# Four k-tile steps for the first projection block, with input quarters and weight halves loaded in turn

## The chip, the cores and the metric

The kernel runs on one core of one Trainium2 chip. The metric is the device time of one execution in microseconds (us). TensorE (PE) does the products and the transposes, with its weight loads shown apart (PEld); VectorE (DVE), ScalarE (ACT) and GpSimd (POOL) do the rest, and SyncE (SP) issues most of the DMAs.

## What is computed

Four layers over a sequence of 256 tokens with 2048 features, all in float32: a mixer of dilated window attention, latent attention (both with a layer norm behind them), and two layers of a second block. Only the very start of the first layer is touched:

```python
cos_a, sin_a = rope_tables(positions, DSA_HEAD_DIM)
h = x @ w_in                                   # (256, 2048) @ (2048, 20480)
qkv = h[..., :3 * DSA_GROUPS * DSA_WIDTH].reshape(B, S, DSA_GROUPS, 3, DSA_HEADS, DSA_HEAD_DIM)
q = apply_rope(qkv[:, :, g, 0], cos, sin)
k = apply_rope(qkv[:, :, g, 1], cos, sin)
o, l = dilated_window_attention(q, k, qkv[:, :, g, 2], window, dilation)
```

## The kernel before

Every product is made of float32 numbers split into a high and a low part: for input and weights alike, `hi` is the rounded copy and `lo` is what is left of the original. The input `x` (tokens on the partitions) is transposed on TensorE into 16 k-tiles of 128 features by 256 tokens. This is `turn_x`: a group g is two k-tiles, so four 128x128 transposes into one bank of the accumulator memory (L660). ACT copies the group to `xh` (L1230) and raises a count, and DVE then makes `xl` (L1810) and raises the count `xt_d`. There are eight groups; two of them come from one quarter of `x`.

Weights come in units of 1 MB, each loaded by two DMAs of 512 KB, its halves, into one of four places of `raw`. A half h goes through `split(h)`: ACT copies it to `whi` (L1200) as soon as the unit is there and place h mod 4 is free (`half_done`), and DVE subtracts to get `wlo` (L1779) and raises `lo_done`. ACT and DVE are three halves ahead of TensorE (`AHEAD`). In the first product of layer 0, `block_by_rows`, a half holds 4 k-tiles of 256 columns: 4 x 2 products with `whi` (L621, 512 wide, against `xh` and `xl` together) and as many with `wlo` (L620, and L623 for the first k-tile). Four halves (0 to 3) make the first block of 16 k-tiles; halves 4 to 7 make the second, and so on. Half h is waited for by `lo_done`, and the first block also waits for `xl` of groups 0 to 3 before half 0 and of groups 4 to 7 before half 2 (L609, L610).

Each engine runs its own program in order; side work is interleaved by hand. A generator (`tables` in the first pair) stands beside the products, and each half lets it take two steps: on TensorE one after two of the four k-tiles and one at the end, on ACT and DVE right behind `split(h + 3)`. The seventh step holds on TensorE the transposes of the vectors (L759, L760), on DVE their copy to `vec` (L1960) and then the whole chain of angles for the rope tables (L1962 to L1990), and on ACT the wait for that chain and the sines (L1348 to L1352). For DVE and ACT the seventh step stands behind `split(6)`. After the sines ACT copies the first block out (L1396), and only then comes `split(7)`. On POOL the seven mask operations (L2536, L2558) wait for the last of DVE's six small mask operations (L2041 to L2044).

At the start SP issues the four quarters of `x` (L562), then eleven small DMAs of rows of vectors (L567), then the weights (L572). TensorE, ACT and DVE do all eight groups of `turn_x`, DVE then the six mask operations, and ACT and DVE then `split(0)` to `split(2)`. The wait of `split(0)` is for both halves of unit 0, since `loaded` counts them together.

Of the kernel before, what the change touches and what calls it, by code (L numbers as in the profile page):

```python
# [10 lines left out]
ALU = mybir.AluOpType  # L11
# [3 lines left out]
P = 128  # L15
# [6 lines left out]
NEG = -1e30  # L22
# [46 lines left out]
def turns(n):  # L69
    for _ in range(n):  # L70
        yield
# [87 lines left out]
def build_program(nc, a, out, layers=(0, 1, 2, 3)):  # L159
    assert tuple(layers) == (0, 1, 2, 3)  # L160
    ctx = ExitStack()
    with ctx:
# [7 lines left out]
        def sem(name):  # L170
            return ctx.enter_context(nc.semaphore(name))

        raw = sb("raw", [P, 4, 4, N])
# [36 lines left out]
        raw_in = [sem(f"raw_in{j}") for j in range(4)]  # L210
        hi_done, lo_done, half_done = sem("hi_done"), sem("lo_done"), sem("half_done")
        x_in = [sem(f"x_in{q}") for q in range(4)]
        x_out = [sem(f"x_out{q}") for q in range(4)]
        vec_in, tab_in = sem("vec_in"), [sem("pos_in"), sem("inv_in")]
        ln_in, l2_in, l3_in = [sem("lng_in"), sem("lnb_in")], [sem("relb_in"), sem("ifb_in")], \
# [6 lines left out]
        m0_g = marks("m0_g", "iota zero band*7")  # L222
        m0_d = marks("m0_d", "bits0 low0 high0 bits1 low1 high1")
        xt_p, xt_a, xt_d = marks("xt_p", "t"), marks("xt_a", "hi"), marks("xt_d", "lo")
# [59 lines left out]
        class L0:  # L284
            c = Carve()
            h = c(10, TB, HALF)
# [13 lines left out]
            bits = flat(t2)[:, 0:S].bitcast(I32)  # L300
# [253 lines left out]

        loaded = [0] * 4
        for n_, (_, parts_) in enumerate(weights()):
            loaded.append(loaded[n_] + 16 * len(parts_))


        def sync(sp):  # L560
            for q in range(4):
                sp.dma_start(x[:, :, q * N:(q + 1) * N],  # L562
                             a["x"][0].rearrange("(t p) d -> p t d", p=P)[:, :, q * N:(q + 1) * N]).then_inc(x_in[q], 16)
            sp.wait_ge(*setup_d.at(0, "zero"))
            for name, src, n in rows:
                g, o = places[name] // P, places[name] % P
                sp.dma_start(vrows[o:o + n, g, :], src).then_inc(vec_in, 16)  # L567
            for u, (_, halves) in enumerate(weights()):
                if u >= 4:
                    sp.wait_ge(lo_done, 2 * (u - 4) + 2)  # L570
                for dst, src in halves:
                    sp.dma_start(dst(raw[:, u % 4]), src).then_inc(raw_in[u % 4], 16)  # L572
            for q in range(4):
                sp.wait_ge(*add_d.at(3, f"add{q}"))
                sp.dma_start(out[0].rearrange("(t p) d -> p t d", p=P)[:, :, q * N:(q + 1) * N],
                             x[:, :, q * N:(q + 1) * N]).then_inc(x_out[q], 16)
            for q in range(4):
                sp.wait_ge(x_out[q], 16)


        def tensor(pe):
# [23 lines left out]
            def block_by_rows(side, bank, wait_x):  # L605


                for u in range(2):
                    if wait_x:  # L609
                        pe.wait_ge(*xt_d.at(4 * u + 3, "lo"))  # L610
                    for s in range(2):
                        h = half[0]
                        pe.wait_ge(lo_done, h + 1)
                        hi, lo = block_half(whi[:, h % 4]), block_half(wlo[:, h % 4])
                        for t in range(4):
                            k = 8 * u + 4 * s + t
                            for c in range(2):
                                cols = slice(c * P, (c + 1) * P)
                                if k:
                                    pe.matmul(ps[:, bank + c, 0:S], lo[:, t, cols], xh[:, k, :], start=False, stop=False)  # L620
                                m = pe.matmul(ps[:, bank + c, :], hi[:, t, cols], xx[:, :, k, :], start=k == 0, stop=k == KT - 1)  # L621
                                if k == 0:
                                    m = pe.matmul(ps[:, bank + c, 0:S], lo[:, t, cols], xh[:, k, :], start=False, stop=False)  # L623
                            if t == 1:
                                next(side, None)
                        m.then_inc(half_done, 1)
                        half[0] += 1
                        next(side, None)
# [34 lines left out]
            def turn_x(layer, groups=range(8)):  # L663
                for g in groups:
                    if layer in (1, 2) or g % 2 == 0:
                        pe.wait_ge(*x_there(layer, g))
                    if g >= 4:
                        pe.wait_ge(*xt_d.at(8 * layer + g - 4, "lo"))
                    four(4 + g % 4, lambda l, tb: x[:, tb, (2 * g + l) * P:(2 * g + l + 1) * P]).then_inc(*xt_p.up("t"))
# [134 lines left out]
                return beside(paced(heads0(pair - 1), 3) if pair else tables_, 54, paced(rope0(pair), 3))  # L804

            pe.wait_ge(*const.at(0, "ident"))
            turn_x(0)
            for pair in range(8):
                side = beside0(pair, tables())
                for s in range(8):  # L810
# [378 lines left out]
        def scalar(act):  # L1189
            half = [0]  # L1190

            def split(h):
                if h >= 2 * len(widths):
                    return
                u = h // 2
                act.wait_ge(raw_in[u % 4], loaded[u + 4])
                if h >= 4:
                    act.wait_ge(half_done, h - 3)
                n = widths[u]
                act.copy(whi[:, h % 4, :, 0:n] if n > FEW else few_high(h, n),  # L1200
                         whole_half(raw[:, u % 4, 2 * (h % 2):2 * (h % 2) + 2], n)).then_inc(hi_done, 1)
# [178 lines left out]
            def beside0(pair, tables_):  # L1380
                return beside(paced(heads0(pair - 1), 3) if pair else tables_, 54, paced(rope0(pair), 3))

            turn_x(0)
            for h in range(AHEAD):
                split(h)
            for pair in range(8):
                side = beside0(pair, tables())
                for s in range(8):
                    b = bank0(s)
                    if s < 6:  # L1390
                        unit(side)
                        unit(side)
                        act.wait_ge(half_done, half[0])
                        if pair:
                            act.wait_ge(*p0_d.at(pair - 1, f"r{s}"))
                        act.copy(L0.h[:, s], ps[:, b:b + 2, 0:S]).then_inc(*e0_a.up(f"out{s}"))  # L1396
                        continue
                    project(side, then=turning_y(0) if pair + s == 14 else None)
                    act.wait_ge(half_done, half[0])
                    if s == 6:  # L1400
                        act.copy(L0.h[:, 6:8].rearrange("p b t c -> p t b c"),
                                 ps[:, b:b + 2, :].rearrange("p t (b c) -> p t b c", b=2)).then_inc(*e0_a.up("out6"))
                    else:
                        if pair:
                            act.wait_ge(*p0_d.at(pair - 1, "z"))
                        act.copy(L0.h[:, 8], ps[:, b:b + 2, 0:HALF])
                        act.activation(L0.h[:, 9], ps[:, b:b + 2, HALF:N], ACT.Copy, scale=0.5).then_inc(*e0_a.up("out7"))
                run(side)
# [361 lines left out]
        def vector(dve):  # L1770
# [184 lines left out]


            def tables():
                yield from turns(6)
                dve.wait_ge(*setup_p.at(0, "vec"))
                dve.tensor_copy(vec[:, :], ps[:, 7, 0:2 * P]).then_inc(*setup_d.up("vec"))  # L1960
                dve.wait_ge(tab_in[0], 16)
# [71 lines left out]
                return beside(paced(heads0(pair - 1), 3) if pair else tables_, 54, paced(rope0(pair), 3))  # L2033

            dve.memset(vrows, 0.0).then_inc(*setup_d.up("zero"))
            turn_x(0)
            dve.wait_ge(*m0_g.at(0, "zero"))
            for i, dil in enumerate((4, 16)):
                if i:
                    dve.wait_ge(*m0_d.at(0, "high0"))  # L2040
                dve.tensor_scalar(L0.bits, L0.iota, dil - 1, None, ALU.bitwise_and).then_inc(*m0_d.up(f"bits{i}"))  # L2041
                dve.wait_ge(*m0_d.at(0, f"bits{i}"))
                dve.tensor_scalar(L0.m0[:, i + 1], L0.bits[:, 0:P], 1.0, NEG, ALU.min, ALU.mult).then_inc(*m0_d.up(f"low{i}"))
                dve.tensor_scalar(L0.m1[:, i + 1], L0.bits, 1.0, NEG, ALU.min, ALU.mult).then_inc(*m0_d.up(f"high{i}"))  # L2044
            for h in range(AHEAD):
                split(h)
            for pair in range(8):
                side = beside0(pair, tables())
                for s in range(8):
                    if s < 6:  # L2050
                        unit(side)
                        unit(side)
                        dve.wait_ge(*e0_a.at(pair, f"out{s}"))
                        dve.tensor_tensor(L0.h[:, s], L0.h[:, s], ps[:, bank0(s):bank0(s) + 2, S:N], ALU.add) \  # L2054
                            .then_inc(*s0_d.up(f"sum{s}"))
                    else:
                        project(side, then=turning_y(0) if pair + s == 14 else None)
                run(side)
# [656 lines left out]
```

## Time and profile before

| what | value |
|---|---|
| median of 3 runs | 2478.17 us (2474.19 to 2478.46) |
| the profiled execution | 2472.55 us |
| its span | 2470.8 us |
| mean granted TensorE clock | 0.995 |
| PE busy | 98% of the span |
| DVE, ACT, POOL busy | 59%, 48%, 6% |

The span runs from the first instruction to the last; 1.75 us of the execution lie around it. Times in the rows are microseconds from the start of the span, durations in a group are means, and what stands in brackets is the idle time of the engine before the row and what ended it. A granted clock of 1.00 is 2.4 GHz and 0.50 is 1.2 GHz.

### The profile page before, as it was taken

The numbers are of one execution on the slowest core, as the hardware profiler recorded it, in microseconds if no ns is written. First come the engines' busy times: TensorE is split into PE (matmuls) and PEld (weight loads), VectorE is DVE, ScalarE is ACT, GpSimd is POOL, SyncE is SP. The second block draws the span as 40 slices with busy tenths as digits, with TensorE's granted clock in tenths as the row PEclk, the third lists the DMA queues.
The fourth block names the chain that finished last, engine by engine and source line by source line (L and its number), as shares of the span: only waits on it lengthen the run. The fifth ranks groups of instructions, "written<-read, shape, count | busy, mean of one in ns | idle before, by whom it ended". The sixth has DMA issues, their size and how long they took to land.

```text
span 2470.8 us, 31396 instructions
## 1 busy us (share of the span) xinstructions
PE 2426.0 (98%) x12674; PEld 2063.6 (84%) x12674; DVE 1469.1 (59%) x1932; ACT 1190.8 (48%) x1620; POOL 152.2 (6%) x127
## 2 busy tenths in 40 slices
PE   8999999999999999989999989999999999999999
PEld 7888888888888888878899878888888887888887
DVE  5757574757475747565556566554455566757654
ACT  4444444444444444445555445555444468655443
POOL 1101010101010101000000000000000010000000
PEclk9999999999999999999999999999999999999999
DMA  7555555545554555546554545555555564433344
GB/s 241 180 174 174 171 183 166 191 160 188 164 191 156 187 163 178 201 142 194 170 137 137 204 147 187 171 187 173 185 169 161 167 205 156 138 116 120 103 137 136
DMA packets 367141, 414.58 MB, mean 168 GB/s; under 512 B 27722, under 2 KB 298276, under 8 KB 366484
## 3 DMA queue, kind: packets, MB, share of 16 engines
q1 hardware_dynamic: 365588, 405.63, 51.5%
q0 software_dynamic: 1408, 6.94, 0.8%
q8 instruction: 100, 1.64, 0.3%
q14 instruction: 45, 0.37, 0.0%
HBM read 410.42 MB, written 2.10 MB: 167 GB/s over the span
## 4 chain that ended last, share of the span: by engine, by line
PE 90%; DVE 4%; ACT 3%; issue 1%; DMA 1%; SPq 0%; POOL 0%; ACTq 0%; DVEq 0%
PE ps L593 18%; PE ps L595 18%; PE ps L594 18%; PE ps L621 14%; PE ps L620 7%; PE ps L1071 2%; DVE wlo L1779 1%; PE ps L660 1%; PE ps L795 1%; ACT whi L1200 1%; PE ps L782 1%; PE ps L787 1%; PE ps L844 1%; PE ps L845 1%; PE ps L846 1%
## 5 line engine op out<-in xcount | busy, mean ns | idle before, releaser
L1779 DVE TENSOR_TENSOR wlo<-raw,whi 128x1024 fp32r<-128x1024 f32 (+1 forms) x768 | 946.7, 1242 | 679.6 <-ACT whi L1200 677.5
L1200 ACT CAST whi<-raw 128x1024 fp32r<-128x1024 f32 (+1 forms) x774 | 801.9, 1041 | 746.9 <-PE ps L595 566.4
L593 PE MATMUL ps<-whi,xx 128*128 128x512 f32 x2112 | 842.1, 399 | 0.7 <-DVE wlo L1779 0.7
L595 PE MATMUL ps<-whi,xx 128*128 128x512 f32 x2112 | 824.0, 390 | 0.0
L594 PE MATMUL ps<-wlo,xx 128*128 128x512 f32 x2112 | 822.6, 389 | 0.0
L621 PE MATMUL ps<-xx,whi 128*128 128x512 f32 x1536 | 540.9, 397 | 5.4 <-DVE wlo L1779 5.4
L595 PEld LDWEIGHTS ps<-whi,xx 128*128 128x128 f32 x2112 | 396.4, 188 | 84.6
L593 PEld LDWEIGHTS ps<-whi,xx 128*128 128x128 f32 x2112 | 396.9, 188 | 79.3 <-DVE wlo L1779 1.4
L594 PEld LDWEIGHTS ps<-wlo,xx 128*128 128x128 f32 x2112 | 397.2, 188 | 77.5
L620 PE MATMUL ps<-xx,wlo 128*128 128x256 f32 x1440 | 406.7, 282 | 0.4 <-DVE wlo L1779 0.4
L621 PEld LDWEIGHTS ps<-xx,whi 128*128 128x128 f32 x1536 | 286.9, 188 | 69.5 <-issue 5.6
L620 PEld LDWEIGHTS ps<-xx,wlo 128*128 128x128 f32 x1440 | 272.2, 189 | 2.9 <-DVE wlo L1779 0.7
L2568 POOL TENSOR_TENSOR work<-work 128x512 f32<-128x512 f32 x48 | 101.7, 2118 | 844.3 <-DVE work L2011 654.8
L1299 ACT ACTIVATE work<-work,small 128x128 f32<-128x128 f32 (+1 forms) x80 | 46.1, 577 | 154.9 <-DVE small L1933 154.9
L2007 DVE TENSOR_TENSOR work<-work 64x512 f32<-64x512 f32 x96 | 88.5, 921 | 2.2
L2054 DVE TENSOR_TENSOR work<-work,ps 128x512 f32<-128x512 f32 x48 | 32.9, 686 | 39.6 <-ACT work L1396 39.6
L1396 ACT COPY work<-ps 128x512 f32<-128x512 f32 x48 | 28.0, 583 | 57.5 <-PE ps L621 57.5
L1071 PEld LDWEIGHTS ps<-work 128*128 128x128 f32 x384 | 49.6, 191 | 7.0 <-DVE work L2414 3.5
L1930 DVE CUSTOM_DVE_ANT_0 work<-ps,work 128x128 f32<-128x128 f32 (+1 forms) x80 | 38.2, 515 | 24.3 <-PE ps L782 18.5
L1071 PE MATMUL ps<-work 128*128 128x128 f32 x384 | 51.1, 276 | 1.4 <-DVE work L2414 1.3
L844 PE MATMUL ps<-xx,whi 128*128 128x256 f32 x160 | 49.0, 306 | 0.0
L846 PE MATMUL ps<-xx,whi 128*128 128x256 f32 x160 | 45.2, 282 | 0.0
(401 smaller groups left out, 1830.5 us busy)
## 6 DMA issues: line engine op xcount, KB each, us to landing
raw<-in_dsa_w_in SPq DMA_DIRECT2D x320, 512.0 KB, 4.5
raw<-in_ev_w_in SPq DMA_DIRECT2D x144, 512.0 KB, 4.6
raw<-in_od_w_in SPq DMA_DIRECT2D x96, 512.0 KB, 4.5
raw<-in_mla_w_in SPq DMA_DIRECT2D x48, 512.0 KB, 4.5
raw<-in_dsa_w_out SPq DMA_DIRECT2D x32, 512.0 KB, 4.6
raw<-in_mla_w_out SPq DMA_DIRECT2D x32, 512.0 KB, 4.8
raw<-in_ev_w_out SPq DMA_DIRECT2D x32, 512.0 KB, 4.5
raw<-in_od_w_out SPq DMA_DIRECT2D x32, 512.0 KB, 4.9
```

The lines of the kernel that those rows point to most:

```text
L593: pe.matmul(o, xh[:, k, tokens[tb]], hi, start=start and s + l == 0, stop=False)
L594: pe.matmul(o, xh[:, k, tokens[tb]], lo, start=False, stop=False)
L595: m = pe.matmul(o, xl[:, k, tokens[tb]], hi, start=False, stop=stop and s + l == 2)
L620: pe.matmul(ps[:, bank + c, 0:S], lo[:, t, cols], xh[:, k, :], start=False, stop=False)
L621: m = pe.matmul(ps[:, bank + c, :], hi[:, t, cols], xx[:, :, k, :], start=k == 0, stop=k == KT - 1)
L844: pe.matmul(o, hi, xh[:, k, :], start=first and g != 1, stop=False)
L846: m = pe.matmul(o, hi, xl[:, k, :], start=False, stop=last and g != 0)
L1071: m = pe.matmul(ps[:, bank, n * P:(n + 1) * P], left[:, n, :], right[:, n, :], start=True, stop=True)
L1200: act.copy(whi[:, h % 4, :, 0:n] if n > FEW else few_high(h, n), whole_half(raw[:, u % 4, 2 * (h % 2):2 * (h % 2) + 2], n)).then_inc(hi_do ...
L1779: dve.tensor_tensor(wlo[:, h % 4, :, 0:n] if n > FEW else few_low(h, n), whole_half(raw[:, h // 2 % 4, 2 * (h % 2):2 * (h % 2) + 2], n), h ...
L2007: m = dve.tensor_tensor(L0.t2[a_], L0.h[b_, n], bc(L0.sina[b_], 1, 2), ALU.mult)
L2568: pool.tensor_tensor(L0.t1, L0.h[:, n], bc(L0.cosa, 1, 2), ALU.mult).then_inc(*p0_g.up(f"cos{n}"))
```

## The change

SP now issues quarter 0 of `x`, half 0 of the weights, quarter 1, half 1, and so on up to half 3, each with a semaphore of its own, then the rows of vectors, then the weights from unit 2 on. `split(0)` to `split(3)` wait for their own half alone. All three engines turn only groups 0 and 1 ahead of the products. TensorE turns groups 2 and 3 after the second k-tile of half 0, groups 4 and 5 after that of half 1, and groups 6 and 7 after that of half 2. ACT and DVE do the same groups right behind `split(0)`, `split(1)` and `split(2)`. TensorE waits for `xl` group by group, before each pair of k-tiles. The six mask operations of DVE go into `tables`: three in its second step, behind `split(3)`, and three in its fourth, behind `split(4)`.

```diff
--- before.py
+++ after.py
@@ -210,6 +210,7 @@
         raw_in = [sem(f"raw_in{j}") for j in range(4)]
         hi_done, lo_done, half_done = sem("hi_done"), sem("lo_done"), sem("half_done")
         x_in = [sem(f"x_in{q}") for q in range(4)]
+        first_in = [sem(f"first_in{h}") for h in range(4)]
         x_out = [sem(f"x_out{q}") for q in range(4)]
         vec_in, tab_in = sem("vec_in"), [sem("pos_in"), sem("inv_in")]
         ln_in, l2_in, l3_in = [sem("lng_in"), sem("lnb_in")], [sem("relb_in"), sem("ifb_in")], \
@@ -554,18 +555,23 @@
 
         loaded = [0] * 4
         for n_, (_, parts_) in enumerate(weights()):
-            loaded.append(loaded[n_] + 16 * len(parts_))
+            loaded.append(loaded[n_] + (16 * len(parts_) if n_ >= 2 else 0))
 
 
         def sync(sp):
-            for q in range(4):
+
+            first = [part for _, halves in list(weights())[0:2] for part in halves]
+            for q, (dst, src) in enumerate(first):
                 sp.dma_start(x[:, :, q * N:(q + 1) * N],
                              a["x"][0].rearrange("(t p) d -> p t d", p=P)[:, :, q * N:(q + 1) * N]).then_inc(x_in[q], 16)
+                sp.dma_start(dst(raw[:, q // 2]), src).then_inc(first_in[q], 16)
             sp.wait_ge(*setup_d.at(0, "zero"))
             for name, src, n in rows:
                 g, o = places[name] // P, places[name] % P
                 sp.dma_start(vrows[o:o + n, g, :], src).then_inc(vec_in, 16)
             for u, (_, halves) in enumerate(weights()):
+                if u < 2:
+                    continue
                 if u >= 4:
                     sp.wait_ge(lo_done, 2 * (u - 4) + 2)
                 for dst, src in halves:
@@ -606,14 +612,14 @@
 
 
                 for u in range(2):
-                    if wait_x:
-                        pe.wait_ge(*xt_d.at(4 * u + 3, "lo"))
                     for s in range(2):
                         h = half[0]
                         pe.wait_ge(lo_done, h + 1)
                         hi, lo = block_half(whi[:, h % 4]), block_half(wlo[:, h % 4])
                         for t in range(4):
                             k = 8 * u + 4 * s + t
+                            if wait_x and t % 2 == 0:
+                                pe.wait_ge(*xt_d.at(k // 2, "lo"))
                             for c in range(2):
                                 cols = slice(c * P, (c + 1) * P)
                                 if k:
@@ -622,6 +628,8 @@
                                 if k == 0:
                                     m = pe.matmul(ps[:, bank + c, 0:S], lo[:, t, cols], xh[:, k, :], start=False, stop=False)
                             if t == 1:
+                                if wait_x and k < 12:
+                                    turn_x(0, (k // 2 + 2, k // 2 + 3))
                                 next(side, None)
                         m.then_inc(half_done, 1)
                         half[0] += 1
@@ -804,7 +812,7 @@
                 return beside(paced(heads0(pair - 1), 3) if pair else tables_, 54, paced(rope0(pair), 3))
 
             pe.wait_ge(*const.at(0, "ident"))
-            turn_x(0)
+            turn_x(0, (0, 1))
             for pair in range(8):
                 side = beside0(pair, tables())
                 for s in range(8):
@@ -1193,7 +1201,10 @@
                 if h >= 2 * len(widths):
                     return
                 u = h // 2
-                act.wait_ge(raw_in[u % 4], loaded[u + 4])
+                if h < 4:
+                    act.wait_ge(first_in[h], 16)
+                else:
+                    act.wait_ge(raw_in[u % 4], loaded[u + 4])
                 if h >= 4:
                     act.wait_ge(half_done, h - 3)
                 n = widths[u]
@@ -1380,9 +1391,10 @@
             def beside0(pair, tables_):
                 return beside(paced(heads0(pair - 1), 3) if pair else tables_, 54, paced(rope0(pair), 3))
 
-            turn_x(0)
+            turn_x(0, (0, 1))
             for h in range(AHEAD):
                 split(h)
+                turn_x(0, (2 * h + 2, 2 * h + 3))
             for pair in range(8):
                 side = beside0(pair, tables())
                 for s in range(8):
@@ -1955,7 +1967,17 @@
 
 
             def tables():
-                yield from turns(6)
+                yield
+                dve.wait_ge(*m0_g.at(0, "zero"))
+                for i, dil in enumerate((4, 16)):
+                    if i:
+                        dve.wait_ge(*m0_d.at(0, "high0"))
+                    dve.tensor_scalar(L0.bits, L0.iota, dil - 1, None, ALU.bitwise_and).then_inc(*m0_d.up(f"bits{i}"))
+                    dve.wait_ge(*m0_d.at(0, f"bits{i}"))
+                    dve.tensor_scalar(L0.m0[:, i + 1], L0.bits[:, 0:P], 1.0, NEG, ALU.min, ALU.mult).then_inc(*m0_d.up(f"low{i}"))
+                    dve.tensor_scalar(L0.m1[:, i + 1], L0.bits, 1.0, NEG, ALU.min, ALU.mult).then_inc(*m0_d.up(f"high{i}"))
+                    yield from turns(2)
+                yield
                 dve.wait_ge(*setup_p.at(0, "vec"))
                 dve.tensor_copy(vec[:, :], ps[:, 7, 0:2 * P]).then_inc(*setup_d.up("vec"))
                 dve.wait_ge(tab_in[0], 16)
@@ -2033,17 +2055,10 @@
                 return beside(paced(heads0(pair - 1), 3) if pair else tables_, 54, paced(rope0(pair), 3))
 
             dve.memset(vrows, 0.0).then_inc(*setup_d.up("zero"))
-            turn_x(0)
-            dve.wait_ge(*m0_g.at(0, "zero"))
-            for i, dil in enumerate((4, 16)):
-                if i:
-                    dve.wait_ge(*m0_d.at(0, "high0"))
-                dve.tensor_scalar(L0.bits, L0.iota, dil - 1, None, ALU.bitwise_and).then_inc(*m0_d.up(f"bits{i}"))
-                dve.wait_ge(*m0_d.at(0, f"bits{i}"))
-                dve.tensor_scalar(L0.m0[:, i + 1], L0.bits[:, 0:P], 1.0, NEG, ALU.min, ALU.mult).then_inc(*m0_d.up(f"low{i}"))
-                dve.tensor_scalar(L0.m1[:, i + 1], L0.bits, 1.0, NEG, ALU.min, ALU.mult).then_inc(*m0_d.up(f"high{i}"))
+            turn_x(0, (0, 1))
             for h in range(AHEAD):
                 split(h)
+                turn_x(0, (2 * h + 2, 2 * h + 3))
             for pair in range(8):
                 side = beside0(pair, tables())
                 for s in range(8):
```

## Rows read from the trace of the kernel before

**Rows 1.** The page: the span, TensorE's busy time, and the chain's shares.
```profile
span 2470.8 us, 31396 instructions
PE 2426.0 (98%) x12674; PEld 2063.6 (84%) x12674; DVE 1469.1 (59%) x1932; ACT 1190.8 (48%) x1620; POOL 152.2 (6%) x127
...
PE 90%; DVE 4%; ACT 3%; issue 1%; DMA 1%; SPq 0%; POOL 0%; ACTq 0%; DVEq 0%
```

**Rows 2.** Timeline, all engines, loads and transposes: start, length, engine, line, count, idle before.
```profile
0.81 1.97 SPq L562 DMA_DIRECT2D x<-in_x  x4
...
5.18 6.07 PE L660 MATMUL ps<-ident,x 128*128 128x128 f32 x32 [5.18 <-DMA x<-in_x]
...
6.30 0.59 ACT L1230 CAST xx<-ps 128x512 fp32r<-128x512 f32 x1 [4.22 <-PE ps L660]
...
7.16 0.59 ACT L1230 CAST xx<-ps 128x512 fp32r<-128x512 f32 x1 [0.27 <-PE ps L660]
7.44 49.48 SPq L572 DMA_DIRECT2D raw<-in_dsa_w_in  x24
...
9.72 2.20 ACT L1230 CAST xx<-ps 128x512 fp32r<-128x512 f32 x4 [0.27 <-PE ps L660]
10.16 0.86 PEld L660 LDWEIGHTS ps<-ident,x 128*128 128x128 f32 x8 [0.21 <-DMA x<-in_x]
```

**Rows 3.** The same timeline from the mask operations to the first products.
```profile
12.74 0.28 DVE L2041 TENSOR_SCALAR work<-work 128x256 int32<-128x256 int32 x1
...
13.99 0.28 DVE L2044 TENSOR_SCALAR work<-work 128x256 f32<-128x256 int32 x1
14.03 1.99 ACT L1200 CAST whi<-raw 128x1024 fp32r<-128x1024 f32 x2 [2.10 <-DMA raw<-in_dsa_w_in]
...
15.11 2.70 DVE L1779 TENSOR_TENSOR wlo<-raw,whi 128x1024 fp32r<-128x1024 f32 x2 [0.83 <-ACT whi L1200]
...
16.61 0.77 PE L621 MATMUL ps<-xx,whi 128*128 128x512 f32 x1 [5.36 <-DVE wlo L1779]
...
19.31 0.41 PE L620 MATMUL ps<-xx,wlo 128*128 128x256 f32 x1
```

**Rows 4.** The same timeline from half 2 to the rope chain's start.
```profile
24.07 1.05 ACT L1200 CAST whi<-raw 128x1024 fp32r<-128x1024 f32 x1 [1.78 <-PE ps L621]
...
26.90 1.05 ACT L1200 CAST whi<-raw 128x1024 fp32r<-128x1024 f32 x1 [1.77 <-PE ps L621]
...
27.98 1.23 DVE L1779 TENSOR_TENSOR wlo<-raw,whi 128x1024 fp32r<-128x1024 f32 x1 [1.59 <-ACT whi L1200]
...
29.12 0.42 DVE L1960 COPY vec<-ps 128x256 f32<-128x256 f32 x1
...
29.44 0.63 PE L621 MATMUL ps<-xx,whi 128*128 128x512 f32 x2
```

**Rows 5.** Timelines of single engines, 36 to 41 us: split(7), half 7, table transposes.
```profile
36.18 3.89 ACT L1200 CAST whi<-raw 128x1024 fp32r<-128x1024 f32 x4
...
37.26 4.63 DVE L1779 TENSOR_TENSOR wlo<-raw,whi 128x1024 fp32r<-128x1024 f32 x4 [0.26 <-ACT whi L1200]
...
38.54 0.38 PE L620 MATMUL ps<-xx,wlo 128*128 128x256 f32 x1 [0.38 <-DVE wlo L1779]
...
40.05 0.60 PE L765 MATMUL ps<-ident,work 128*128 128x128 f32 x4
...
40.68 0.37 ACT L1358 COPY work<-ps 128x256 f32<-128x256 f32 x1 [0.62 <-PE ps L765]
```

**Rows 6.** The POOL masks, from the timeline: start, length, count.
```profile
14.50 3.82 POOL L2536 TENSOR_SCALAR_AFFINE_SELECT work<-work 128x128 f32<-128x128 f32 x6 [10.01 <-DVE work L2044]
```

**Rows 7.** Stretches: busy time of PE, PEld, DVE, ACT, POOL; granted clock; DMA share; GB/s.
```profile
13.00:14.00 1.00, 0.00 (x0) 0.00 (x0) 0.90 (x6) 0.00 (x0) 0.00 (x0) 0.54 1.09 348
...
19.00:20.00 1.00, 1.00 (x5) 0.82 (x5) 1.00 (x2) 0.02 (x1) 0.66 (x1) 0.54 1.10 348
```

## The prediction

> **What bounds the kernel.** I read the page first: TensorE is busy 2426.0 of 2470.8 us and holds 90% of the chain that ended last [rows 1]. So only what delays TensorE counts, and almost all of the span is untouched. Next I read the timeline of the start. TensorE waits 5.18 us for the first quarter, transposes until 11.25, and then waits 5.36 us for its first product at 16.61 [rows 2, 3]. In that wait ACT idles 2.10 us for the weights, which are there at 14.03 [rows 3]. The change aims at this stretch. The reader should then look for the next place where TensorE is not fed: half 7 starts at 38.54, 0.38 us late, when `wlo` of `split(7)` is there [rows 5]. Behind that start stand, in DVE's and ACT's program order, `split(6)` at 27.98, the copy of the vectors at 29.12, the rope chain, the sines, and `split(7)` [rows 4, 5]. A time saved on TensorE before half 7 is thus worth something only if DVE also gets to the rope chain earlier; a delay of `split(6)` passes to half 7 almost in full. I count the change to that start, since from there the program and its covers are the same as before.
>
> **Loads.** Eight groups of transposes take quarters at 5.18 and, for the last, at 10.16 where TensorE waited 0.21 for it: (10.16 - 5.18) / 3 = 1.66 us for 512 KB [rows 2]. In the new order half 0 of the weights lands near 5.18 + 1.66 = 6.8, quarter 1 near 8.5, half 1 near 10.2, quarter 2 near 11.8, half 2 near 13.5, quarter 3 near 15.1 and half 3 near 16.8. SP issued a quarter each 0.5 us (four in 1.97), so the eight go out by 5 us, ahead of the engines that carry them [rows 2]. The eleven row loads go from before the weights to behind half 3; they are wanted first in half 3, about 12 us after half 3's data is there, and unit 2 is issued behind them at about the 9.5 us at which it went out before. I count the loads at nothing from here on; the cover is the slow sequence of the engines, worked out next. The four extra semaphores cost no instruction.
>
> **First product.** The casts of groups 0 and 1 stay at 6.30 and 7.16 [rows 2]. `split(0)` follows at the pitch of casts in a row, (2.20 - 0.59) / 3 = 0.54 us, at 7.70 [rows 2]. DVE starts 15.11 - 14.03 = 1.08 after it and takes 1.23 us without POOL beside it [rows 3, 4], and TensorE begins 0.1 later: 7.70 + 1.08 + 1.23 + 0.1 = 10.1 against 16.61. That is 6.5 us gained. It is almost all lost again, because in the old order half 1, 2 and 3 were ready without TensorE's help, and in the new one they are not.
>
> **Each round from half to half.** ACT's program now has groups 2 and 3 ahead of `split(1)`, and these wait for TensorE to do two k-tiles of half 0 first. So half 1 can start only after this string, of which nothing lies beside the next: two k-tiles, two groups of transposes, ACT's casts of them, ACT's `split(1)`, DVE's `split(1)`. The same holds for halves 2 and 3. At 2.4 GHz: a half takes 26.90 - 24.07 = 2.83, so two k-tiles 1.42 [rows 4]. A group's transposes take 0.86 / 2 = 0.43 [rows 2]; a cast follows the first of four transposes by 40.68 - 40.05 = 0.63 [rows 5], so the second group's cast starts at the later of 0.43 + 0.63 and 0.63 + 0.54, 1.17. `split` follows 0.54 later, DVE 1.08 after that, 1.23 long, 0.1 to TensorE: 1.17 + 0.54 + 1.08 + 1.23 + 0.1 = 4.12. One round is 1.42 + 4.12 = 5.54 us for 2.83 us of products. DVE's `xl` (0.69 each, its rows as the casts') lies beside ACT's `split`, at no cost.
>
> The first round is at 1.2 GHz, at least in its beginning: the first two k-tiles took 19.31 - 16.61 = 2.70 [rows 3], groups of transposes come 7.16 - 6.30 = 0.86 apart, the first cast 6.30 - 5.18 = 1.12 after the first transpose [rows 2]. All at that clock: 2.70 for the k-tiles and 1.12 + 0.86 + 0.54 + 1.08 + 1.23 + 0.1 = 4.93 behind them, 7.63. The clock granted at 13.0 to 14.0 fell to half, 1.8 us after the transposes ended, and rose at about 19.9, 3.3 us after the first product [rows 3, 7]. TensorE is busy without a pause from 10.1 in the new order, so a rise 3.3 us in, at 13.4, spares most of the slow transposes. 7.63 is the upper end and 7.63 - (4.93 - 4.12) = 6.82 the lower; I take 7.3. Starts: half 1 at 17.4, half 2 at 22.9, half 3 at 28.5. With half 3's products (2.83) and the two transposes of vectors (0.2), the first block ends at 31.5; before it ended at 29.44 [rows 4].
>
> **DVE on its way to the rope chain.** `split(3)` ends 0.1 before half 3, at 28.4. Before, the first six halves' splits had been done early, and `split(6)` only waited for its place. Now DVE has in a row: three mask operations, `split(4)`, three mask operations, `split(5)`, `split(6)`. Six mask operations took 13.99 + 0.28 - 12.74 = 1.53 [rows 3], which used to lie in the wait for weights and now lie on this path; a split in a row takes (4.63 - 1.23) / 3 = 1.13 [rows 5]. `split(6)` starts at 28.4 + 1.53 + 2 x 1.13 = 32.2. The end of the mask operations also starts POOL's masks, 3.82 us for six [rows 6]; beside them DVE's splits took 2.70 / 2 = 1.35 or more instead of 1.23 [rows 3], which adds 0.1 to 0.3 here. `split(6)` comes 32.4 - 27.98 = 4.4 later than before. The chain, the sines, and `split(7)` follow as before, so half 7 starts 4.4 to 4.6 later, near 43.0. TensorE is through half 6 at 31.5 + 3 x 2.83 = 40.0, so it waits 3.0 us there; the first block's own lateness (2.1) lies inside. After it ACT and DVE split four in 3.89 and 4.63 us against 11.3 us of products and are ahead again [rows 5]. I see nothing later that gives back or adds.
>
> **Sum.** +4.5 us. Bounds: 3.7 (early rise of the clock, no cost of POOL) to 5.9 (late rise, and one round with a clock that has fallen, worth 2.70 - 1.42 = 1.3 in its k-tiles and less in its transposes). On the profiled execution that is 2472.55 + 4.5 = 2477.1; on the median of the runs shown, which lies 5.6 above it, 2478.17 + 4.5 = 2482.7. Median and profiled execution differ by more than the effect, and the profile is the lowest of the four executions, so I forecast near the median's figure, 2482.
>
> **Rivals.**
> (a) The clock falls in every round. TensorE idles 4.12 - 0.86 - 1.42 = 1.8 us of each 5.54, just as long as the time from the end of the transposes to the fall seen at 13 us [rows 2, 7]; for it speaks this, against it that products of 2.8 us lie between. A slow round costs (2.70 - 1.42) + (4.93 - 4.12) = 2.1 more; rounds 2 and 3 give 4.2, so 4.5 + 4.2: 2486.9. The Trainium skill has such a rule in TensorE: Matmul & The Clock Gate, section "HAM oscillation — how this bites in real kernels": bursts too short beside their waits make every tile of a loop start throttled. No row here shows an alternation; the rule and this trace agree only in that a wait lowered the clock.
> (b) Loads don't come in turn. If the queue's transfers share the engines, so that half 0 of the weights is there only with the last quarter or later, at 14 instead of 6.8, the first product goes back to 16.6 and the rounds come on top. It decides from a landing later than 7.7. Quarters in the trace landed 1.66 apart in order of issue, which speaks against it [rows 2]. Time: + 4.5 + 6.3, 2489.
> (c) The change does what it is meant to: rounds are hidden and TensorE runs on. Then the first block is 29.44 - 16.61 = 12.83 of work, plus six groups, two at 0.86 and four at 0.43, 3.4 us: it ends at 10.1 + 12.8 + 3.4 = 26.3, 3.1 early; the rope chain starts as much earlier: 2475.1. It needs ACT to split half 1 before groups 2 and 3, and its program order says otherwise.
> (d) Only the block's lateness counts, +2.1, 2480.3, if DVE makes up its mask operations and splits before the rope chain. DVE has no idle time there in my sum, so it's unlikely.
>
> **How the numbers follow.** Forecast 0.62, (a) 0.10, (b) 0.06, (c) 0.12, (d) 0.10. A measurement of this kernel can tell about 0.2%, 5.0 us, from no change. The forecast at +3.7 to +5.9 straddles that edge: 0.26 of its 0.62 to slower. Slower: 0.26 + 0.10 + 0.06 = 0.42. Faster needs more than (c) gives and mostly luck in the runs: 0.07. Same: 0.51. Leaving out (b), with some of (a) and the lower part of (c), and with 2 us for the spread of the runs, the range is 2476 to 2488.
>
> **What would show it.** Right: ACT's `split(0)` at 7.7; first product near 10.1; casts of groups 2 and 3 right ahead of `split(1)`; halves 1 to 3 starting some 5.5 us apart with TensorE idle 1.7 to 1.9 before each; first block's end near 31.5; the vectors' copy near 33.5; a wait of some 3 us before half 7, and half 7 near 43. Wrong: ACT casting a half while TensorE is still in its first two k-tiles of the one before, or half 7 starting before 39.

## The result and the profile after

The changed kernel takes 2480.01 us (median of 19 runs, 2476.52 to 2482.26) against 2476.23 us for the kernel before (19 runs beside them, 2471.95 to 2478.47). The ratio is 1.0016, 95% interval 1.0009 to 1.0022: 3.8 us slower, between 2.2 and 5.4. The profiled execution took 2480.01 us, its span 2478.3. The forecast of the median, near 2482, was +4.5 us on the 2478.17 of three runs; over 19 runs that median is 2476.23, and the interval of the difference holds 4.5.

Line numbers moved by a few: the transposes are L668, ACT's casts of `x` L1241 and of weights L1211, DVE's `xl` L1822 and `wlo` L1791, the products L627, L626 and L629, and the copy of the vectors L1982.

The timeline of the changed kernel from the first group to half 3, all engines (start, length, engine, line, count, idle time before and what ended it):

```profile
5.47 1.94 PE L668 MATMUL ps<-ident,x 128*128 128x128 f32 x8 [5.47 <-DMA x<-in_x]
...
7.93 1.05 ACT L1211 CAST whi<-raw 128x1024 fp32r<-128x1024 f32 x1
...
9.01 1.23 DVE L1791 TENSOR_TENSOR wlo<-raw,whi 128x1024 fp32r<-128x1024 f32 x1 [0.25 <-ACT whi L1211]
...
10.29 0.80 PE L627 MATMUL ps<-xx,whi 128*128 128x512 f32 x1 [2.88 <-DVE wlo L1791]
...
14.11 0.58 ACT L1241 CAST xx<-ps 128x512 fp32r<-128x512 f32 x1 [5.13 <-PE ps L668]
...
14.96 0.59 ACT L1241 CAST xx<-ps 128x512 fp32r<-128x512 f32 x1 [0.27 <-PE ps L668]
...
15.44 1.05 ACT L1211 CAST whi<-raw 128x1024 fp32r<-128x1024 f32 x1
...
17.80 0.39 PE L626 MATMUL ps<-xx,wlo 128*128 128x256 f32 x1 [0.78 <-DVE wlo L1791]
...
23.28 0.39 PE L626 MATMUL ps<-xx,wlo 128*128 128x256 f32 x1 [1.54 <-DVE wlo L1791]
...
28.75 0.39 PE L626 MATMUL ps<-xx,wlo 128*128 128x256 f32 x1 [1.54 <-DVE wlo L1791]
```

The first product is at 10.29 instead of 16.61 [rows 3]. But halves 1, 2 and 3 start at 17.80, 23.28 and 28.75, each after a wait for `wlo`. In the row at 14.11 ACT has idled 5.13 us for TensorE's transposes, and only behind the two casts does it come to half 1, at 15.44.

From half 3 to half 7, DVE's and TensorE's own timelines:

```profile
28.61 0.29 DVE L1975 TENSOR_SCALAR work<-work 128x256 int32<-128x256 int32 x1
...
31.08 2.45 DVE L1791 TENSOR_TENSOR wlo<-raw,whi 128x1024 fp32r<-128x1024 f32 x2
33.45 0.41 DVE L1982 COPY vec<-ps 128x256 f32<-128x256 f32 x1
...
34.74 0.37 DVE L1994 TENSOR_SCALAR work<-work 128x192 f32<-128x192 f32 x1
```

```profile
31.65 0.63 PE L627 MATMUL ps<-xx,whi 128*128 128x512 f32 x2
...
43.24 0.39 PE L626 MATMUL ps<-xx,wlo 128*128 128x256 f32 x1 [2.72 <-DVE wlo L1791]
```

The first block ends at 31.65 against 29.44, the vectors are copied at 33.45 against 29.12 [rows 4], and half 7 starts at 43.24 against 38.54 [rows 5], 4.70 us late, after a wait of 2.72. Behind that wait the clock fell. The stretches of the changed kernel (columns as in rows 7; the first figure after POOL's is the granted clock):

```profile
43.00:44.00 1.00, 0.76 (x4) 0.70 (x5) 1.00 (x2) 1.00 (x2) 0.00 (x0) 0.83 0.00 0
44.00:45.00 1.00, 1.00 (x5) 0.81 (x5) 1.00 (x2) 0.77 (x1) 0.00 (x0) 0.50 0.57 140
...
46.00:47.00 1.00, 1.00 (x6) 1.00 (x5) 0.59 (x1) 0.27 (x2) 0.00 (x0) 0.50 1.09 387
47.00:48.00 1.00, 1.00 (x7) 0.83 (x7) 0.00 (x0) 0.38 (x2) 0.54 (x1) 0.96 1.10 362
```

**A mark for all traces.** The medians scatter by more than the terms in question, so I read each trace at one more place: the first transposes of layer 1. Nothing edited here runs later. TensorE's timeline, the kernel before and then the changed one:

```profile
1081.70 1.11 PE L660 MATMUL ps<-ident,x 128*128 128x128 f32 x4 [5.24 <-DVE x L1887]
```

```profile
1088.13 1.12 PE L668 MATMUL ps<-ident,x 128*128 128x128 f32 x4 [5.24 <-DVE x L1899]
```

The mark is 6.43 us later: 4.70 until half 7 and 1.73 from there on.

### The profile page after: what moved, and what is told of

Read it like the earlier page. It is cut to its first block, busy times and chain, and to the rows that moved or that the text cites. A ratio compares the mean times of both kernels' runs of the same rounds, so it can differ in the third digit from the quotient of the medians.

```text
span 2478.3 us, 31398 instructions
## 1 busy us (share of the span) xinstructions
PE 2429.8 (98%) x12674; PEld 2067.7 (83%) x12674; DVE 1468.9 (59%) x1932; ACT 1190.1 (48%) x1620; POOL 150.7 (6%) x127
## 4 chain that ended last, share of the span: by engine, by line
PE 90%; DVE 4%; ACT 3%; issue 1%; DMA 1%; POOL 0%; DVEq 0%; ACTq 0%
PE ps L599 18%; PE ps L601 18%; PE ps L600 18%; PE ps L627 14%; PE ps L626 7%; PE ps L1079 2%; PE ps L668 2%; DVE wlo L1791 2%; PE ps L803 1%; ACT whi L1211 1%; PE ps L790 1%; PE ps L795 1%; PE ps L852 1%; PE ps L853 1%; PE ps L854 1%
## 5 line engine op out<-in xcount | busy, mean ns | idle before, releaser
L1791 DVE TENSOR_TENSOR wlo<-raw,whi 128x1024 fp32r<-128x1024 f32 (+1 forms) x768 | 946.2, 1241 | 675.7 <-ACT whi L1211 673.4
L1211 ACT CAST whi<-raw 128x1024 fp32r<-128x1024 f32 (+1 forms) x774 | 801.8, 1041 | 739.3 <-PE ps L601 567.7
L627 PE MATMUL ps<-xx,whi 128*128 128x512 f32 x1536 | 543.0, 399 | 2.9 <-DVE wlo L1791 2.9
L626 PE MATMUL ps<-xx,wlo 128*128 128x256 f32 x1440 | 409.1, 284 | 6.6 <-DVE wlo L1791 6.6
L627 PEld LDWEIGHTS ps<-xx,whi 128*128 128x128 f32 x1536 | 288.4, 189 | 66.8 <-DVE wlo L1791 3.3
L626 PEld LDWEIGHTS ps<-xx,wlo 128*128 128x128 f32 x1440 | 273.3, 190 | 10.1 <-DVE wlo L1791 7.8
```

The lines of the kernel that those rows point to most:

```text
L1791: dve.tensor_tensor(wlo[:, h % 4, :, 0:n] if n > FEW else few_low(h, n), whole_half(raw[:, h // 2 % 4, 2 * (h % 2):2 * (h % 2) + 2], n), h ...
```

## The experiments

Shifts are against the trace of the kernel before (half 7 at 38.54, mark at 1081.70). Each ratio is against runs of the kernel before made beside it. The changed kernel has 19 runs, `xfirst` 5 and the others 8 to 11. The three second traces are at the end; that of the kernel before has its half 7 0.72 us and its mark 0.61 us later than the first, so shifts of that size are within the scatter of single traces.

| kernel | first product | first block ends | half 7 (wait before it) | shift of half 7 | shift of the mark | ratio (95%) |
|---|---|---|---|---|---|---|
| before | 16.61 | 29.44 | 38.54 (0.38) | | | |
| changed | 10.29 | 31.65 | 43.24 (2.72) | +4.70 | +6.43 | 1.0016 (1.0009 to 1.0022) |
| order | 10.42 | 26.81 | 38.81 (3.15) | +0.27 | +1.80 | 1.0010 (1.0001 to 1.0019) |
| masks | 10.28 | 31.66 | 41.44 (0.92) | +2.90 | +2.85 | 1.0015 (1.0006 to 1.0024) |
| rope | 10.19 | 31.13 | no wait | | +1.22 | 1.0008 (0.9999 to 1.0016) |
| xfirst | 14.14 | 35.52 | 47.10 (2.72) | +8.56 | +11.37 | 1.0038 (1.0025 to 1.0052) |
| ordermasks | 10.22 | 27.01 | 37.49 (1.75) | -1.05 | -1.03 | 0.9983 (0.9974 to 0.9992) |
| all | 10.24 | 25.85 | no wait | | -4.08 | 0.9982 (0.9974 to 0.9991) |
| loads | 21.45 | 35.46 | 44.58 (0.39) | +6.04 | +6.35 | 1.0019 (1.0010 to 1.0028) |
| longwait | 16.50 | 29.11 | 41.85 (3.88) | +3.31 | +5.90 | 1.0023 (1.0013 to 1.0033) |

**The splits one half further ahead (order).** On ACT and DVE alike:

```diff
             turn_x(0, (0, 1))
-            for h in range(AHEAD):
-                split(h)
-                turn_x(0, (2 * h + 2, 2 * h + 3))
+            split(0)
+            split(1)
+            turn_x(0, (2, 3))
+            split(2)
+            turn_x(0, (4, 5))
...
                     split(half[0] + AHEAD)
+                    if half[0] == 0:
+                        turn_x(0, (6, 7))
```

> The changed kernel with ACT and DVE one half further ahead of the turning: groups 0 and 1, split(0), split(1), groups 2 and 3, split(2), groups 4 and 5, split(3), groups 6 and 7. Nothing else differs. Theory (the rounds through ACT and DVE cost the time): half 1 no longer waits behind TensorE's turning of groups 2 and 3; halves 1, 2 and 3 start back to back, at about 16.9, 20.6 and 24.3 us; the first block ends near 27.3 instead of 31.8; half 7 starts near 36 to 38 instead of 43.2; the median is 4 to 7 us below the changed kernel and 1 to 3 us below the kernel before. Rival (the loads or the clock, not the order of the splits, set the starts of the halves): starts stay at 17.8, 23.3 and 28.7, and the time stays.

TensorE ran from half 0 to the end of half 6 without one wait, and the first block ended at 26.81, 4.8 us before the changed kernel's. So the rounds are the order of ACT's and DVE's programs, not loads or clock. The rest of the expectation missed: half 7 was at 38.81, not 36 to 38, the mark 1.80 late, and the median 3.1 us above the kernel before and not 1 to 3 below it. The gain went into the next wait, and behind that wait the clock fell, from about 39.5 to 42.9 us; that is the 1.5 us between the two shifts. DVE's timeline, the second three mask operations, two splits, the copy of the vectors, and TensorE's row of half 7:

```profile
25.98 0.28 DVE L1981 TENSOR_SCALAR work<-work 128x256 int32<-128x256 int32 x1
26.30 0.23 DVE L1983 TENSOR_SCALAR work<-work 128x128 f32<-128x128 int32 x1
26.45 0.28 DVE L1984 TENSOR_SCALAR work<-work 128x256 f32<-128x256 int32 x1
26.65 2.44 DVE L1795 TENSOR_TENSOR wlo<-raw,whi 128x1024 fp32r<-128x1024 f32 x2
29.01 0.41 DVE L1988 COPY vec<-ps 128x256 f32<-128x256 f32 x1
```

```profile
38.81 0.39 PE L626 MATMUL ps<-xx,wlo 128*128 128x256 f32 x1 [3.15 <-DVE wlo L1795]
```

The stretch behind it, with a granted clock of 0.76:

```profile
39.00:40.00 1.00, 1.00 (x6) 0.85 (x6) 1.00 (x2) 1.00 (x2) 0.00 (x0) 0.76 0.13 22
```

The first block is 2.6 us earlier than in the kernel before, and the copy at 29.01 only 0.1.

**DVE's mask operations first (masks).**

```diff
             dve.memset(vrows, 0.0).then_inc(*setup_d.up("zero"))
+            dve.wait_ge(*m0_g.at(0, "zero"))
+            for i, dil in enumerate((4, 16)):
+                ...
...
             def tables():
-                yield
-                dve.wait_ge(*m0_g.at(0, "zero"))
-                ...
-                yield
+                yield from turns(6)
```

> The changed kernel with DVE's six mask operations put ahead of its first groups, where it waits for the first transposes. Theory: they lie on the path to the rope chain and are 1.5 us of the 4.7 by which half 7 is late, and POOL's masks beside the splits another 0.1 to 0.3. Half 7 starts at 41.4 to 41.8 instead of 43.2, the median is 1.5 to 2 us below the changed kernel. Rival (the copy of the vectors is what waits, or DVE had slack there): half 7 at 43.2, the same time.

Half 7 at 41.44 with the first block's end unmoved (31.66): the mask operations, with POOL's masks behind them, were worth 1.80 us. Of these 1.43 lie ahead of the copy of the vectors (32.02 instead of 33.45): twice 0.67 for three operations each, and 0.1 on the splits. The other 0.37 lie in the rope chain and what follows it, which take 9.42 us from the copy to half 7 instead of 9.79. The chain's first operations are shorter here; this is the row that is at 34.74 in the changed kernel:

```profile
33.12 0.26 DVE L1984 TENSOR_SCALAR work<-work 128x192 f32<-128x192 f32 x1
```

In the changed kernel POOL's masks run from 31.38 to 35.37, beside these operations. The longer way, 9.79 to 9.80 us, is in all traces with the mask operations in `tables` and a wait before half 7, and the 9.4 in those with them earlier, longwait with its added copies aside. That POOL's masks are what lengthens it is read from these coincidences; no run moves POOL's masks alone. The wait of 0.92 left the clock up, and the mark shows the same shift as half 7. The median does not show the gain: it is 4.2 us above that of the kernel before, as far as the changed kernel's within the intervals.

**ACT's wait for the rope chain four steps later (rope).**

```diff
             def tables():
-                yield from turns(6)
+                yield from turns(10)
                 act.wait_ge(*rope_d.at(0, "end"))
...
-                yield from turns(7)
+                yield from turns(3)
                 act.wait_ge(*rope_p.at(0, "tab"))
```

> The changed kernel with ACT's wait for the rope chain and the sines four steps later, behind split(8) instead of split(6); DVE's chain stays. Theory: half 7 waits only because split(7) stands behind chain and sines; it then starts when TensorE is through half 6, near 40.3, and the granted clock does not fall at 44 us. The shift against before is the first block's lateness alone, about 2 us; the median is 3 to 4 us below the changed kernel. Rival (the wait of half 7 is made up later or hides something else, such as the loads): half 7 earlier but the time within 1 us of the changed kernel.

No wait before half 7 and no fall of the clock. The first block ended 31.13 - 29.44 = 1.69 late, the 0.38 us wait of the kernel before is gone, and the mark is 1.22 late. This is the rival "only the block's lateness counts", made true by an edit. The median was 2.4 us above the kernel before, so 1.4 nearer to it than the changed kernel's, and not the 3 to 4 that I expected; the interval holds both.

**All quarters ahead of the weight halves (xfirst).** SP issues the four quarters, then the four halves, rows still behind.

```diff
-            for q, (dst, src) in enumerate(first):
+            for q in range(4):
                 sp.dma_start(x[:, :, q * N:(q + 1) * N], ...).then_inc(x_in[q], 16)
+            for q, (dst, src) in enumerate(first):
                 sp.dma_start(dst(raw[:, q // 2]), src).then_inc(first_in[q], 16)
```

> The changed kernel with the four quarters issued ahead of the four weight halves, as before; rows still behind them. Theory (what the change wins is the early start of half 0, and the rounds cost the same wherever they start): first product at 14.2 instead of 10.3, rounds of 5.5 us after it, half 7 near 47; the median 3.5 to 4.5 us above the changed kernel. Rival (the rounds take that long only because quarters and halves of weights come in turn): halves start closer to each other than 5.5 us and the time is that of the changed kernel or less.

The first product was at 14.14, the halves after it at 21.66, 27.14 and 32.62: rounds of 7.52, 5.48 and 5.48 again, though all of `x` was there. So the rounds do not come from the loads. The early start is worth 8.56 - 4.70 = 3.9 us, and the changed kernel keeps it; it is paid for behind.

**Order and masks together (ordermasks).**

> As before but with ACT's wait for the rope chain in its old step: only the further split ahead and the early mask operations. Theory: the vectors' copy at about 27 instead of 29.0 in the run with the order alone; half 7 near 36.5, after a wait of 0.9 us that leaves the clock up; layer 1's first transposes 2.0 us earlier than in the kernel before. Rival (the mask operations had been hidden in the order run, where half 2 frees the place of split(6) only late): copy at 29.0, half 7 at 38.8, as in the order run.

The copy of the vectors came at 28.08 and half 7 at 37.49 after 1.75 us of waiting, without a fall of the clock. The mark is 1.03 earlier than before, half of what I expected: the copy came 0.93 earlier than in the run with the order alone, and not 2.0. DVE's timeline:

```profile
23.23 1.29 DVE L1828 TENSOR_TENSOR xx<-ps,xx 128x512 fp32r<-128x512 f32 x2 [1.02 <-ACT xx L1243]
24.67 3.50 DVE L1795 TENSOR_TENSOR wlo<-raw,whi 128x1024 fp32r<-128x1024 f32 x3
```

The `xl` of the last two groups starts at 23.23, 0.25 later than with the order alone, as the clock had risen later behind the first product. Behind it DVE cannot start half 4 before ACT's cast of it, which starts at 23.57 and takes 1.05; some 0.2 us of the mask operations had lain in that gap. The rival had said that all of them were hidden, by the place of `split(6)`. That place is no limit here: half 2 is through near 24.2, and ACT casts halves 4, 5 and 6 without a wait, the last from about 25.5.

**All three edits (all).**

> The changed kernel with three edits together: ACT and DVE one half further ahead of the turning, the six mask operations at DVE's very start, and ACT's wait for the rope chain four steps later. Theory (rounds, mask operations and the rope chain's place are all that stood against the early start): first product 10.3, halves follow without idle time, half 7 starts near 35.6 with no wait before it. The first transposes of layer 1, 1081.70 in the kernel before, start near 1078.8, and the median is about 3 us below the kernel before. Rival (something else at the start takes its place, as loads of unit 2 or the places of the split halves): TensorE waits between halves 3 and 7 and the gain is under 1 us.

TensorE has two waits in its first 55 us, for the first quarter and for half 0:

```profile
5.41 1.94 PE L668 MATMUL ps<-ident,x 128*128 128x128 f32 x8 [5.41 <-DMA x<-in_x]
10.24 0.79 PE L627 MATMUL ps<-xx,whi 128*128 128x512 f32 x1 [2.88 <-DVE wlo L1795]
```

The mark is at 1077.62, 4.08 earlier than in the kernel before (2.9 expected), and the median is 2472.67 against 2477.04 us. This version and ordermasks are faster than both kernels of the case. The medians do not show the step from ordermasks to this version: they differ by 0.6 us, and the marks by 3.05. ACT's row for half 1 shows a wait for a load, as in the two other versions with this order; TensorE did not wait for it:

```profile
10.88 1.04 ACT L1211 CAST whi<-raw 128x1024 fp32r<-128x1024 f32 x1 [1.95 <-DMA raw<-in_dsa_w_in]
```

**The order of loads alone (loads).** The kernel before with SP's program, the semaphores and ACT's waits of the change; all groups are turned ahead of the products.

> The kernel before with the new order of loads alone: quarters and weight halves in turn, rows behind; all eight groups are still turned ahead of the products. Theory: the last quarter lands near 15.1 instead of 10.1, and groups 6 and 7, the mask operations and split(0) follow it: first product near 21.2 instead of 16.61, half 7 near 43.1, layer 1's first transposes 4.6 us later. The loads' order alone costs; it pays only with the turning beside the products. Rival (only the weights' landing counts, and it moves from 14.0 to 10.2 for the first unit): first product at 16.6 or earlier.

The first product was at 21.45 as expected (21.2), half 7 at 44.58 and not 43.1. TensorE's timeline shows each pair of groups waiting for its quarter, of which this is the last:

```profile
15.40 1.97 PE L666 MATMUL ps<-ident,x 128*128 128x128 f32 x8 [0.95 <-DMA x<-in_x]
```

The first block took 14.0 us instead of 12.8, since the products with `wlo` stayed at 0.41 us each for 6.2 us, against 3.3 in the kernel before, and then went to 0.28; and the mark is 6.35 late instead of 4.6.

**A longer wait before half 7 in the kernel before (longwait).**

```diff
                 act.wait_ge(*rope_d.at(0, "end"))
+                act.wait_ge(*const.at(0, "nhalf"))
+                for i in range(24):
+                    act.copy(small[:, 208 + 2 * i:210 + 2 * i], nhalf[:, 0:2])
```

> The kernel before with 24 tiny copies added on ACT between the rope chain and the sines, and nothing else; they lengthen the wait before half 7 from 0.38 to some 3 us (2.6 to 3.6). Theory (a wait of this length before half 7 lets the clock fall to 1.2 GHz soon after, whatever made the wait): layer 1's first transposes are later than before by more than half 7 is, by 0.5 to 2 us; the clock of some 3 us behind half 7 is 0.5. Rival (the fall at 44 us in the changed kernel belongs to its uneven first block): no fall, both shifts the same.

```profile
33.26 2.34 ACT L1346 COPY small<-nhalf 128x2 f32<-128x2 f32 x24 [5.62 <-DVE work L1993]
35.60 1.28 ACT L1351 ACT_TABLE_LOAD   x1
```

The wait grew to 3.88 us, more than I had aimed at, since ACT's table load of 1.28 us, which had been hidden in the wait for the rope chain, now came behind the copies. The clock was 0.50 from about 40, inside the wait, to about 47 us. Half 7 is 3.31 late, the mark 5.90: 2.6 us come from the clock, more than the 0.5 to 2 that I expected, in a kernel whose first block is the old one.

**Second traces.** Two of the changed kernel, one of the kernel before.

> The changed kernel once more, unedited, for a second trace. Theory: everything up to the wait before half 7 is where it was, within what the moment of the clock's rise in the first half moves (0.7 us); half 7 at 42.5 to 43.3 after a wait of 2.7 us; whether the clock falls behind it differs from execution to execution, so layer 1's first transposes stand 4.0 to 6.6 us behind those of the kernel before (1081.70). That would square the 6.4 us of the first trace with the 3.8 us between the medians. Rival: the fall is there each time and the 6.4 us too.

> As look_a, a third trace of the changed kernel; the same expectations.

> The kernel before once more, unedited, for a second trace. Theory: the clock falls in the wait for the first weights and rises 3.3 to 6.8 us after the first product; the trace of before has the earliest rise, so this one stands level or up to 1.7 us later at layer 1's first transposes: 1081.6 to 1083.4. Rival (the kernel before has no scatter there): 1081.7 within 0.1.

TensorE's rows at half 7 and at the mark, first look_a, then look_b:

```profile
43.03 0.39 PE L626 MATMUL ps<-xx,wlo 128*128 128x256 f32 x1 [2.87 <-DVE wlo L1791]
...
1086.13 1.11 PE L668 MATMUL ps<-ident,x 128*128 128x128 f32 x4 [5.23 <-DVE x L1899]
```

```profile
43.09 0.58 PE L626 MATMUL ps<-xx,wlo 128*128 128x256 f32 x1 [2.87 <-DVE wlo L1791]
...
1089.00 1.12 PE L668 MATMUL ps<-ident,x 128*128 128x128 f32 x4 [5.24 <-DVE x L1899]
```

The same wait of 2.87 us left the clock up in look_a (shifts +4.49 and +4.43) and lowered it for 6.8 us in look_b (+4.55 and +7.30, which is above the 6.6 I had allowed). The kernel before moved by 0.61 at the mark (1082.31), its clock having risen 5.0 us after the first product instead of 3.3. Its half 7 was at 39.26.

## Why the prediction was right, point by point

**The early first product** was forecast at 10.1 and is at 10.29: the first quarter landed at 5.47 instead of 5.18, and `split(0)` had its weights before its turn.

**The rounds** were forecast at 7.3, 5.54 and 5.54 us and took 7.51, 5.48 and 5.47. The run with the order changed removed them whole, and the one with all of `x` there kept them. So the step "ACT's program has the next groups ahead of the next split, and these wait for TensorE" is shown.

**DVE's way to the rope chain** was forecast to bring `split(6)` and the copy 4.4 later; the copy came 4.33 later. The masks' part, 1.53 and 0.1 to 0.3, measured 1.80. But the parts are not those of the sum: the operations themselves took 1.34, and of the 0.46 from POOL's masks only 0.1 lies on the splits. The rope chain, counted "as before", took the 0.37 more. That these errors cancel is luck. **Half 7** was put at 43.0 and started at 43.24, 43.03 and 43.09 in three traces, after 2.7 to 2.9 us of waiting instead of 3.0.

**A term was missing.** I wrote that I saw nothing later that gives back or adds. The wait of 3 us that I had forecast before half 7 itself could lower the clock, which I had weighed only for the rounds, as rival (a). In the rounds, with waits of 0.8 to 1.6 us, the clock stayed up in each of the six traces that have them. Behind half 7 it fell in two of three, for 1.7 and 2.8 us. The upper bound of 5.9 held one such fall and was passed at the mark twice. The longer wait in the old kernel shows that a wait at this place is enough to lower the clock, whatever the first block was like.

**The rule from the skill** (the Trainium skill, TensorE: Matmul & The Clock Gate, section "HAM oscillation — how this bites in real kernels") describes a loop whose work per tile is shorter than the wait behind it. The rounds had 3.9 us of work beside waits of 1.5, and the clock stayed up, so they do not test that rule. That a single wait can lower the clock the traces show: it fell at waits of 2.72 to 3.88 us in five of them, and stayed up at one of 2.87 us (look_a) and one of 1.75 (ordermasks).

**Other rivals.** (b) fell: no split of the changed kernel waited for its load. (c) was right about the end of the first block, 26.3 against 26.81 in the run with the order changed, and wrong about this program. With that order alone the mark is still 1.8 us late; with the early mask operations too the gain there is 1.0 us, and 4.1 with the rope chain's wait moved as well. (d) did not come true here, since DVE had no idle time to make up for the splits; it came true with the rope chain's wait moved. My claim that unit 2 is issued at about 9.5 as before was wrong: SP's issues grew longer (up to 2.15 us for one row load), and it came at 12.98. It cost nothing, as nothing waited for it.

**What stays open.** The three traces of the changed kernel average 6.1 us at the mark over the first trace of the kernel before, and 5.7 over the mean of its two; the medians differ by 3.8 (2.2 to 5.4). From the mark to the end the thirteen traces take 1389.1 to 1394.5 us, whatever the kernel, and in those that take over 1392 the mean granted clock from 1470 us on is 0.99 instead of 1.00. That is as large as the effect, and three traces are too few to say how often half 7's fall comes. The half-7 shift of 4.5 to 4.7 (4.2 between the means of three and of two traces) lies in the interval of the medians, the 6.43 of the first trace does not. Within one kernel the time follows the mean granted clock of the run: of the 19 runs of the changed kernel the seven fastest (2476.52 to 2478.53) had 0.996 or 0.997, and the eleven that took 2479.93 or more had 0.993 to 0.995.

## What to carry to other kernels

When a step is moved beside the products, read the program of every engine that serves it: work placed ahead of the next weight split makes that split wait for TensorE, and the overlap turns into rounds. Small operations taken out of an idle stretch are not free in the new place. Before counting a gain at the start, follow it to the next place where the bound engine is fed late; here a first product 6.3 us earlier came with a half 7 that was 4.7 us later, and the mark was earlier than before only once the path to half 7 was shortened too.

## What the runs showed of the hardware

- The granted clock of a stretch reads 1.00 until the first change on record, also where TensorE ran at 1.2 GHz. The changed kernel's first product took 0.80 us at a recorded 1.00 (the stretch from 10 to 11 us), as the 0.77 of the kernel before at 0.50 [rows 3]. Only the durations tell it.
- Waits of the same 2.87 us in the same kernel lowered the clock once and once not. TensorE had been busy for over 11 us before each.
- SP took 2.15 us to issue a load of 48 KB that had taken 0.52, with eight loads of 512 KB queued ahead of it instead of four; in the run `loads`, with the same eight ahead, it took 1.46:

```profile
6.59 2.15 SPq L571 DMA_DIRECT2D y<-in_od_conv_d_w  x1
...
12.98 44.33 SPq L578 DMA_DIRECT2D raw<-in_dsa_w_in  x18
```
